# Seven quarter products in place of eight for the gate and up blocks of the three largest experts

## The reference, cut to what matters

```python
def swiglu(t, wg, wu, wd):
    return (jax.nn.silu(t @ wg) * (t @ wu)) @ wd

def moe_swiglu(h, router_w, wg, wu, wd):        # 512 tokens, width 1024
    ...
    top_logits, top_idx = lax.top_k(logits, 2)  # two of 8 experts for each token
    top_w = jax.nn.softmax(top_logits, axis=-1)
    ...
    for e in range(8):                          # expert width 1408
        y = y + gates[:, e:e + 1] * swiglu(t, wg[e], wu[e], wd[e])
```

## Time and profile before

| | us |
|---|---|
| median of 3 runs | 1947.34 (1946.88 to 1947.86) |
| the profiled execution | 1949.36 |
| its span, first to last instruction | 1947.4 |
| PE busy in the span | 1913.6 (98%) |
| DVE, ACT, POOL busy in the span | 869.7, 566.9, 680.9 |
| expert blocks, first weight DMA of rank 0 to the end | 1361.3 to 1947.4 |

### The profile page before, as it was taken

The page is one execution under the profiler, slowest core; times in us unless marked ns, Lnnn a source line. Parts: engine busy times, 40 slices in busy tenths (PEclk is TensorE's granted clock), DMA queues, the critical chain, the costliest instruction groups (busy, mean ns, idle before and its releaser), DMA issues. The chain is left out here.

```text
span 1947.4 us, 36158 instructions
## 1 busy us (share of the span) xinstructions
PE 1913.6 (98%) x14812; PEld 1596.7 (82%) x14812; DVE 869.7 (45%) x1177; ACT 566.9 (29%) x1210; POOL 680.9 (35%) x590
## 2 busy tenths in 40 slices
PE   9999999999999999999999999999999999999997
PEld 8778645888746888888877888745999999999996
DVE  4898587667425444444436777732200000000023
ACT  1443213455512111110036657532120210111102
POOL 5755432655414444444526777520300000000011
PEclk9999999999999999999999999999999999999999
DMA  9214750322224666631211111101967578778893
GB/s 334 86 55 154 281 186 22 101 83 73 82 65 152 215 216 212 211 130 60 102 67 67 67 66 64 59 12 48 313 214 254 195 243 268 257 263 334 334 353 146
DMA packets 82822, 313.54 MB, mean 161 GB/s; under 512 B 10122, under 2 KB 10642, under 8 KB 82530
## 3 DMA queue, kind: packets, MB, share of 16 engines
q1 hardware_dynamic: 75952, 289.73, 42.2%
q0 software_dynamic: 4464, 14.35, 2.1%
q10 hardware_dynamic: 2241, 7.14, 1.0%
HBM read 301.43 MB, written 9.75 MB: 160 GB/s over the span
## 5 line engine op out<-in xcount | busy, mean ns | idle before, releaser
L259 PE MATMUL banks<-sb_act,sb_ring 128*64 128x112 f32 (+10 forms) x5184 | 686.1, 318 | 1.9 <-DMA sb_ring<-in_w_moe_up 1.0
L259 PEld LDWEIGHTS banks<-sb_act,sb_ring 128*128 128x128 f32 (+1 forms) x5184 | 598.9, 173 | 80.1 <-issue 66.5
L259 PE MATMUL banks<-sb_x_norm,sb_ring 128*128 128x256 f32 (+3 forms) x1616 | 330.9, 403 | 3.2 <-ACT sb_ring L466 2.3
L259 PEld LDWEIGHTS banks<-sb_x_norm,sb_ring 128*128 128x128 f32 (+1 forms) x1616 | 242.6, 171 | 66.0 <-issue 29.6
L3455 DVE TENSOR_TENSOR sb_act<-sb_work,banks 128x192 f32<-128x192 f32 (+7 forms) x88 | 27.2, 309 | 485.4 <-PE banks L259 478.3
L441 POOL TENSOR_TENSOR sb_ring<-sb_ring 128x512 f32<-128x512 f32 x146 | 206.4, 1414 | 104.7 <-PE banks L259 54.3
L259 PE MATMUL banks<-sb_work,sb_ring 128*128 128x256 f32 (+2 forms) x1028 | 220.6, 410 | 1.9 <-ACT sb_ring L466 1.8
L259 PEld LDWEIGHTS banks<-sb_work,sb_ring 128*128 128x128 f32 (+1 forms) x1028 | 147.9, 168 | 53.2 <-issue 32.7
L2986 POOL DMA_INDIRECT sb_work<-first_expert_rows,sb_table x8 | 7.5, 936 | 441.6 <-DMA first_expert_rows<-sb_x_norm 439.5
L3257 ACT ACTIVATE sb_work<-banks 128x192 f32<-128x192 f32 (+7 forms) x88 | 25.7, 294 | 296.4 <-PE banks L259 294.4
L497 POOL TENSOR_TENSOR sb_act<-sb_act,sb_ring 128x256 f32<-128x256 f32 x75 | 71.8, 958 | 69.4 <-ACT sb_act L466 61.9
(11 more groups left out here) (501 smaller groups left out, 2459.2 us busy)
## 6 DMA issues: line engine op xcount, KB each, us to landing
sb_ring<-in_w_moe_up SPq DMA_DIRECT2D x176, 512.0 KB, 4.9
sb_ring<-in_w_moe_down SPq DMA_DIRECT2D x64, 704.0 KB, 6.2
sb_act<-in_cond_w SPq DMA_DIRECT2D x84, 512.0 KB, 3.8
sb_ring<-in_w_ffn_up SPq DMA_DIRECT2D x44, 512.0 KB, 5.2
sb_ring<-in_w_h_in SPq DMA_DIRECT2D x32, 512.0 KB, 4.1
sb_ring<-in_w_in SPq DMA_DIRECT2D x28, 512.0 KB, 5.5
sb_ring<-in_w_m_in SPq DMA_DIRECT2D x24, 512.0 KB, 4.0
sb_ring<-in_w_ffn_down SPq DMA_DIRECT2D x16, 704.0 KB, 5.6
```

Source lines behind the costliest of these rows:

```text
L259: last = m.nc.tensor.matmul(out[part], weights[:, part], act, start=start, stop=stop, skip_group_check=skip)
```

## The change

For rank 0 from pair 4 on, and for ranks 1 and 2 in all 11 pairs, the gate block (b11 on its first 4 input tiles, b21 on the last 4) and the up block (b12, b22) are multiplied together. The columns of the expert are cut into two halves of h = 96, 92 or 80. With weight differences t1 to t4 and input sums s1 to s4 there are seven products, each of 4 steps with 128 weights columns by h moving columns, in place of eight such products before. They run in the order P1, P7, P6, P2, P5, P4, P3 in three PSUM banks.

- POOL makes t1 = b12 - b11 (128x512). Its 9 gathers are now issued one after each of the first 9 such differences.
- DVE makes t3 = b22 - b12 (over b12), t2 = b22 - t1 and t4 = b21 - t2 (128x512 each), four input sums for each rank (128x(4h)), the sums c11 (bank + kept part), c22 (bank + kept part) and c21 (bank + kept part), and the product with Silu in two halves: the high half from SBUF, the low half straight from the bank of the last product.
- ACT copies three partial results out of PSUM (h columns each) besides Silu of all columns, which now reads `gated` in SBUF. The result copies of the rank before are cut into up to four parts, one in each of pairs 2 to 5.
- PE waits for the kept parts, the differences and the sums between its products. `m.strip` is 64 for all pairs and, with them, for the down blocks of ranks 0, 1 and 2.
- `blocks_done` grows by 2 at the end of a pair and no longer by 1 after each block.
- `silu_t` moves to another place in the same tensor; the differences live in tensors that are free in this stage.

```diff
+    direct = [4] + [0] * (EXPERTS - 1)
+    paired = 3
+    quick = [(r, j) for r in range(paired) for j in range(direct[r], KE)]
+    number = {pair: n for n, pair in enumerate(quick)}
...
+    t_two, t_others = four(m.spare[:, 0, :]), (four(m.spare[:, 1, :]), m.sgw[:],
+                                               four(m.pw[:].rearrange("p a c -> p (a c)")))
+    differences = lambda n: (t_others[n % 3], t_two, t_others[(n - 1) % 3])
+    banks_of = lambda n, r: [ps[:, bank, 0:half(r)] for bank in ((0, 1, 2), (2, 1, 0))[n % 2]]
...
+    dve_order = []
+    for n, (r, j) in enumerate(quick):
+        ahead = (r, j + 1) in number
+        dve_order += [(n, "t3"), (n, "t2"), (n, "t4")] if j == direct[r] else []
+        dve_order += [(n + 1, "t3"), (n + 1, "t2")] if ahead else []
+        dve_order += [(n, "c11"), (n, "c22")]
+        dve_order += [(n + 1, "t4")] if ahead else []
+        dve_order += [(n, "c21")]
+    made_no = {name: past["added"] + i + 1 for i, name in enumerate(dve_order)}
...
-                for i in range(first_pass(p), GATHERS):
+
+                def fetch(i):
...
+                for n in range(len(quick)):
+                    combine(n)
+                    if n + 1 < GATHERS:
+                        fetch(n + 1)
...
+            def combine(n):
+                r, j = quick[n]
+                b11, b12, b21, b22 = quarters(j)
+                t1, t2, t4 = differences(n)
+                wait_weights(pool, r, j)
+                if n >= 2:
+                    pool.wait_ge(products, product_no(n - 2, P4))
+                give(pool, nc.gpsimd.tensor_tensor(t1, b12, b11, ALU.subtract), combined, combined_no(n))
...
-                    m.strip = 64 if cap < P else P
+                    m.strip = 64 if cap < P or first_pass(p) and 0 < r < paired else P
...
+            def pair(r, j):
+                m.strip = 64
+                n, base, h = number[r, j], r * total + done, half(r)
+                first = j == direct[r]
+                b11, b12, b21, b22 = (lambda k, w=w: w[:, k, :] for w in quarters(j))
+                t1, t2, t4 = (lambda k, w=w: w[:, k, :] for w in differences(n))
+                s1, s2, s3, s4 = (lambda k, w=w: w[:, k, :] for w in sums_of(r))
+                act = xT[:, :, FIRST[r]:FIRST[r] + CAPS[r]]
+                a11, a12, a22 = (lambda k, f=f, c=c: act[:, f + k, c:c + h] for f, c in ((0, 0), (HK, 0), (HK, h)))
+                r1, r2, r3 = banks_of(n, r)
+                wait_weights(pe, r, j)
+                if first:
+                    pe.wait_ge(m.evac, base + (2 * j - 2 if j else -1))
+                if n:
+                    pe.wait_ge(made_by_dve, made_no[n - 1, "c11"])
+                multiply(m, r1, HK, b11, a11).then_inc(products, 1)
+                if first:
+                    pe.wait_ge(m.evac, base + 2 * j)
+                    pe.wait_ge(inputs, inputs_no(r, S3))
+                if n:
+                    pe.wait_ge(made_by_dve, made_no[n - 1, "c21"])
+                pe.wait_ge(made_by_dve, made_no[n, "t3"])
+                multiply(m, r2, HK, b12, s3).then_inc(products, 1)
+                if first:
+                    pe.wait_ge(inputs, inputs_no(r, S2))
+                pe.wait_ge(made_by_dve, made_no[n, "t2"])
+                pe.wait_ge(partials, partial_no(n, OF_1))
+                multiply(m, r1, HK, t2, s2, onto=True).then_inc(products, 1)
+                pe.wait_ge(m.evac, base + 2 * j)
+                multiply(m, r3, HK, b21, a12).then_inc(products, 1)
+                pe.wait_ge(partials, partial_no(n, OF_16))
+                multiply(m, r1, HK, t1, s1, onto=True).then_inc(products, 1)
+                pe.wait_ge(made_by_dve, made_no[n, "t4"])
+                multiply(m, r2, HK, t4, a22, onto=True).then_inc(products, 1)
+                if first:
+                    pe.wait_ge(inputs, inputs_no(r, S4))
+                pe.wait_ge(made_by_dve, made_no[n, "c22"])
+                multiply(m, r1, HK, b22, s4, onto=True).then_inc(m.blocks_done, 2)
+
...
+                def keep(r, j):
+                    n, base = number[r, j], r * total + done
+                    of_1, of_7, of_16, of_165 = parts_of(r)
+                    r1, r2, r3 = banks_of(n, r)
+
+                    def take(part, bank, i, product, free=None):
+                        if n and free:
+                            act.wait_ge(made_by_dve, made_no[n - 1, free])
+                        act.wait_ge(products, product_no(n, product))
+                        nc.scalar.activation(part, bank, ACT.Copy).then_inc(partials, 1)
+
+                    take(of_1, r1, OF_1, P1, "c11")
+                    take(of_7, r2, OF_7, P7, "c22")
+                    take(of_16, r1, OF_16, P6, "c21")
+                    if r and 2 <= j < 6:
+                        take_result_part(r - 1, j - 2)
+                    act.wait_ge(m.evac, base + 2 * j)
+                    act.wait_ge(made_by_dve, made_no[n, "c21"])
+                    nc.scalar.activation(silu_t[j % 2][:, 0:CAPS[r]], gated[:, 0:CAPS[r]], ACT.Silu).then_inc(silu, 1)
 
...
+            def add_inputs(r):
+                h, act, (s1, s2, s3, s4) = half(r), xT[:, :, FIRST[r]:FIRST[r] + CAPS[r]], sums_of(r)
+                a11, a12, a21, a22 = act[:, 0:HK, 0:h], act[:, HK:, 0:h], act[:, 0:HK, h:], act[:, HK:, h:]
+                made = lambda a, b, out, op, which: give(dve, nc.vector.tensor_tensor(out, a, b, op), inputs,
+                                                         inputs_no(r, which))
+                made(a11, a21, s3, ALU.subtract, S3)
+                made(a21, a22, s1, ALU.add, S1)
+                made(s1, a11, s2, ALU.subtract, S2)
+                made(a12, s2, s4, ALU.subtract, S4)
+
+            def combine(n, which):
+                r, j = quick[n]
+                b11, b12, b21, b22 = quarters(j)
+                t1, t2, t4 = differences(n)
+                if which == "t3":
+                    dve.wait_ge(combined, combined_no(n))
+                    give(dve, nc.vector.tensor_tensor(b12, b22, b12, ALU.subtract), made_by_dve, made_no[n, "t3"])
+                elif which == "t2":
+                    if n:
+                        dve.wait_ge(products, product_no(n - 1, P6))
+                    give(dve, nc.vector.tensor_tensor(t2, b22, t1, ALU.subtract), made_by_dve, made_no[n, "t2"])
+                else:
+                    if n:
+                        dve.wait_ge(products, product_no(n - 1, P5))
+                    give(dve, nc.vector.tensor_tensor(t4, b21, t2, ALU.subtract), made_by_dve, made_no[n, "t4"])
+
+            def add_parts(r, j):
+                n, base, h, cap = number[r, j], r * total + done, half(r), CAPS[r]
+                of_1, of_7, of_16, of_165 = parts_of(r)
+                r1, r2, r3 = banks_of(n, r)
+                ahead = (r, j + 1) in number
+                made = lambda a, b, out, name: give(dve, nc.vector.tensor_tensor(out, a, b, ALU.add), made_by_dve,
+                                                    made_no[n, name])
+                if ahead:
+                    combine(n + 1, "t3")
+                    combine(n + 1, "t2")
+                dve.wait_ge(products, product_no(n, P2))
+                dve.wait_ge(partials, partial_no(n, OF_1))
+                made(r3, of_1, gated[:, 0:h], "c11")
+                dve.wait_ge(products, product_no(n, P5))
+                dve.wait_ge(partials, partial_no(n, OF_16))
+                made(r1, of_7, of_165, "c22")
+                if ahead:
+                    combine(n + 1, "t4")
+                dve.wait_ge(products, product_no(n, P4))
+                made(r2, of_16, gated[:, h:cap], "c21")
+                dve.wait_ge(silu, r * KE + j + 1)
+                nc.vector.tensor_tensor(hid[:, j, h:cap], silu_t[j % 2][:, h:cap], of_165, ALU.mult).then_inc(m.evac, 1)
+                dve.wait_ge(m.blocks_done, base + 2 * j + 2)
+                nc.vector.tensor_tensor(hid[:, j, 0:h], silu_t[j % 2][:, 0:h], r1, ALU.mult).then_inc(m.evac, 1)
+
+            def start_pairs(r):
+                n = number[r, direct[r]]
...
+            dve.wait_ge(x0_out, KD)
+            add_inputs(0)
             dve.wait_ge(exp_out, 1)
...
+                        if first_pass(p) and (r, j) in number:
+                            if j == direct[r]:
+                                start_pairs(r)
+                            add_parts(r, j)
+                            continue
...
+                    if first_pass(p) and r + 1 < paired:
+                        dve.wait_ge(turned_out, need[r + 1] - 1)
+                        add_inputs(r + 1)
```

More of the change, by code:

```diff
@@ L2872, in stage_moe @@
     rows_of = lambda r: out_rows[r % 2][0].rearrange("p a c -> p (a c)")
[L2873 removed]
+    flat_w = W[:].rearrange("p a c -> p (a c)")
+    late_w = 16 * S
+    silu_t = [flat_w[:, late_w + i * CAP:late_w + (i + 1) * CAP] for i in range(2)]
     out_rows = [(m.HN[:, 4 * i:4 * i + 2, :], m.HN[:, 4 * i + 2:4 * i + 4, :]) for i in range(2)]
```

(48 more changed lines are left out.)

14 lines of the change are left out of this document (13 added, 1 removed).

## The result

| | before | after |
|---|---|---|
| median of 6 runs each, us | 1947.6 (1946.64 to 1948.87) | 1953.52 (1950.53 to 1956.24) |
| the profiled execution, its span | 1949.36, 1947.4 | 1955.48, 1953.6 |
| first weight request of rank 0 | 1361.28 | 1358.76 |

The ratio is 1.0024, with a 95% interval from 1.0014 to 1.0035. The change makes the kernel slower by 5.9 us in the medians and by 4.7 us by the ratio; 1943.5 was forecast. The runs after also lie over twice as far apart as those before (5.7 us against 2.2).

The account below looks back on a forecast made before the run. PE's rate bounds the kernel; after the change PE bounds ranks 0 and 1, DVE rank 2. Pair gains 10.2 - start 5.8 - clock 0.3 - first P7 waits 0.3 = 3.8; 1947.34 - 3.8 = 1943.5 us; own range 1941.5 to 1946, with rivals 1938.5 to 1951.5.

Parts of the forecast that it names:

- PE's own work: Paired blocks: couples of strips at 83, 79.5 and 69.5 ns, pairs of 4.65, 4.45, 3.89 us; PE alone saves 14.7 us.
- No floor: PE in paired blocks: short matmuls can start every 29 ns, under the 35 ns needed at h = 80.
- The rival that came nearest: PE's weight loads bind in pairs: 97 ns a couple of strips, 5.43 us a pair, 1972 us in all; chance 0.02.
- the prediction's fit: PE matmul time in pairs: 0.83 ns a column plus 3 ns, giving 69.5 ns a couple of strips at h = 80.
- the store of the result: ACT, result of the rank before: copies in parts ahead of a Silu not due for 1.5 us, costing nothing.
- the start: Rank 0's first pairs: PE waits 4.5 us for POOL's table and t1, then again before P3; 5.8 us, between 4.3 and 7.
- its clock: PE's granted clock may fall after 4.5 us of rest in rank 0: 0.3 us, bounds 0 and 3.
- rank 2's period: Rank 2 becomes bound by DVE at 4.24 us a pair, from 4.35; gain 1.2 us over 11 pairs.
- DVE's circle with POOL's turn: DVE's work per pair, with POOL's difference holding up the high product by 0.68 us: 4.31, 4.28, 4.23 us.
- the rival in which POOL's turn hides: POOL's difference hides under c11, c22 and DVE's waits; PE bounds rank 2 at 4.02 us; 1939.5 us, chance 0.27.
- The first rival: POOL's difference runs before t4, making pairs 4.75, 4.72, 4.67 us if in all three ranks; 1951.3 us, chance 0.19.
- The second wait: Rank 0's first pair: PE waits before P3 for c22, delayed on DVE, 1.05 us.

## Why the prediction was wrong

**The step that failed** stands in "PE's own work": "Is there a floor for so short instructions? ... No floor." Rows 5 show that PE can start an instruction each 29 ns, and no run speaks against it: in the pairs it started one each 37 to 42 ns. But the row was of 16 instructions. Whether PE is *given* instructions at this rate for 128 us of pairs (7 x 4.67 + 11 x 4.51 + 11 x 4.15) is another question, and nothing in the sum asked it. The prediction counted 112 matmuls a pair and gave the number a price in PE's time, none in bytes. The rival that came nearest, that PE would be bound by weight loads, did not happen: couples of strips ran at 83, 80.5 and 74 ns (the undisturbed periods below over 56), all under the 97 that it assumed. At 80 columns the 74 is above the 69.5 of the prediction's fit, so the fit was 6% short there.

**The missing term** is 8.4 us of late instructions (9.7 from start to start) and 1.7 us of clock behind the longest. The forecast of the ranks was 3.8 saved and this execution lost 8.8, 12.6 apart. Of that 9.7 + 1.7 = 11.4 is this term. Narrow strips around the transposes cost 0.6 and 0.5 us in ranks 1 and 2, as in the run with strips of 64, and a product that waited for ACT's kept part (L3378) lost 0.3 in rank 1 and 0.5 in rank 2. The 0.5 is the store of the result, which the prediction put at nothing; it counted the copies and not the 2.5 us in which ACT issues their DMAs (1566.85 to 1569.31). Against these 1.9 us the start was 0.5, its clock 0.3 and rank 2's period 11 x 0.09 = 1.0 us better than forecast. 11.4 + 1.9 - 1.8 = 11.5 leaves about 1 us open. Each profiled execution has its own stalls: the medians are 5.9 us apart, the runs after spread over 5.7 us.

**The gains of an undisturbed pair were right.** These pairs take 4.67, 4.51 and 4.15 us, for 4.66, 4.50 and 4.24. The 4.24 of rank 2 came near for the wrong reason. It was DVE's circle with POOL's turn, but POOL's turn hides under DVE's wait for Silu, and in undisturbed pairs of rank 2 PE waits for nobody. There the rival in which POOL's turn hides was right, but PE's own bound lay at 4.15 and not at 4.02; a circle taken too long and a bound taken too short nearly made up for each other, which is luck. The first rival, POOL ahead of t4, didn't happen: in rank 2 POOL started 0.17 to 0.35 us after t4, and t4 stayed at 0.69.

**The start was right in sum, not in its parts.** The whole stage ran 2.5 us earlier in this execution, and with it the table's landing, at about 1388.9. PE stood still 3.3 us from start to start, not 4.5: DVE's first product, behind the input sums, had already held it back by 0.6 at pair 2, which the stall gave back as forecast, and POOL began 0.4 sooner after the start of the stage than taken. The second wait was 1.4 in place of 1.05. Together 0.6 + 3.3 + 1.4 = 5.3 against 5.8. Taking most of it away brought 3.7 us in the medians. The clock did not fall there: it stayed at 1.00 from 1385 to 1395. It fell where the prediction had not looked, after the long stall in rank 2.

**Not tried:** whether an earlier or a smaller fetch, or weight loads in smaller pieces or spread otherwise, would let the fetch through. That the packet waits in the queues of the DMA engines behind the weights fits all runs, but its own request is not in the trace, so how long it stood there was not seen.

## What to carry to other kernels

Count the instructions that an edit adds, not only their time: each 256 of PE's are one 16 KB packet that shares the DMA engines with the data. Beside 512 KB weight loads one packet each 7 to 12 us was in time in the one profiled execution that had it, and at one each 4 to 6 us in all three ranks PE stood still for 4.9 to 8.4 us of the profiled executions; here fewer multiplications in shorter pieces cost more than they saved. An idle time that the profile gives to "issue", that ends in the middle of a product and some 2.4 us after an instruction packet began, was in all these runs a late packet; the sure sign is that PE's instructions between two such times are a multiple of 256.

## What the runs showed that was not expected

- PE, in straight code without a branch, stood still up to 2.7 us for its instructions. The Trainium skill ("Runtime: NRT & Kernel Launch", section Instruction fetch mechanics) says that the fetch is hidden by the pace at which instructions are issued, and that crossing a 16 KiB boundary is mostly hidden. The block size agrees (16384 bytes a packet); the hiding does not hold at 37 to 42 ns a matmul, each with its weight load, beside 240 GB/s on the DMA engines: 8.4 us were not hidden.
- From the start of the packet to PE's next instruction it is 2.2 to 2.5 us, though the packet takes only 0.9 to 1.0; in no run did PE begin on a packet sooner than 2.2 us after its start.
- Only one packet is kept ahead. Since the stalls tell which instruction is the first of a packet, the others can be counted from them: between 1366 and 1612 us of the kernel before each packet starts 232 to 291 PE instructions ahead of its own first one, and no packet of any run over 296 ahead. In the dense stretches (1400 to 1428, 1463 to 1507 and 1549 to 1595 us) the changed kernel has a median of 140, with quarter loads 183; strips of 32 have 183, with quarter loads 217. So the fetch starts later, counted in instructions, when PE runs them faster, and earlier again when the weight traffic goes. An estimate from that: with 4.7 to 5.3 us of instructions in a packet, one that starts over some 2.5 to 3 us late is felt; with 10 us, nearly 8 us are allowed. Strips of 64 agree: there the latest packet started 6.2 us before its first instruction ran, and nothing stalled.
- The granted clock halved for 3.4 us after stalls of 2.9 us (1576.81 in the kernel after) and 2.8 us (1377.22 with strips of 32), but not after the one of 3.3 us that ended at 1391.05, before which PE had run at full clock with long matmuls. Why it did not there is open.
- Quarter loads changed ranks 0 to 2 of the kernel before by nothing at all: 76.82, 85.64, 76.66 us both times.
